# The weight sums of the second feed-forward matmul: DMA adds into the raw tiles in SBUF in place of sums kept in device memory

## Chip, cores, metric

One core of one Trainium2 chip runs the whole program. The metric is device microseconds for one execution; the times given are medians of repeated runs. The engines are TensorE (PE: matmuls, PEld: its weight loads), VectorE (DVE), ScalarE (ACT), GpSimd (POOL) and SyncE (SP). DMAs are issued by SyncE, ACT or GpSimd and carried out by 16 DMA engines.

## What is computed

One decoder block on 512 tokens of width 1024 in float32: normalisation, one input projection, sparse attention beside a gated channel mixer, an output projection with residual, and then the feed-forward part that the change is about:

```python
h = rms_norm(x, g_ffn_norm[l])
x = x + jnp.square(jax.nn.relu(h @ w_ff1[l])) @ w_ff2[l]
```

`w_ff1` is 1024 x 4096, `w_ff2` 4096 x 1024. The output is the new `x`.

## The kernel before

**Precision.** TensorE multiplies in a reduced format, so each operand is split in a high and a low part and each product is three matmuls (`three`, lines 354 to 358: high by high, high by low, low by high). ACT makes the high part with a copy, VectorE the low part by subtracting it from the raw value.

**First feed-forward matmul.** 32 hidden tiles of 128 rows, 24 matmuls each, weights streamed by SyncE into `raw`, four slots of 128x1024. ACT applies the relu from PSUM (`relu`, lines 1012 to 1016), VectorE squares (`square`, line 1529) and makes three sums of the activations of a K-tile pair (`sums`, lines 1536 to 1539). The activations lie in `aq`, six forms of 256 tokens each: A11, S1, A22, S2, A12, A21.

**Second feed-forward matmul.** It is a Strassen-like scheme: K and the tokens are cut in halves, and instead of eight block products there are seven, P1 to P7, of sums of blocks. 16 K-tiles of each half are paired. For a pair k the stored weights `w_ff2[k, 0:4]` are four 128x512 pieces (their signs are such that all sums are additions). With w0 to w3 for them, P1 uses w0, P5 w0+w1, P6 w0+w1+w2, P4 w0+w1+w2+w3, P3 w2, P7 w1+w2, P2 w3. A product has two PSUM banks, one for each 128 tokens: P1 and P2 banks 0 and 1, P5 and P3 2 and 3, P6 and P7 4 and 5, P4 6 and 7.

The sums of weights are made by GpSimd's DMA queue in device memory, in the tensor `forms` (five pieces for a pair): `form_step` (line 570) issues seven DMAs for a pair, three copies and four adding ones, each waiting for the one before on the same pair; two pairs, even and odd, take turns. They start once the mixer's norms are done and run beside attention and the first feed-forward matmul. SyncE then loads the tiles from `forms` or `w_ff2` (`first_group`, `second_group`, lines 464, 472, 475). In step J of the first group one pair is used for P1, P5, P6 and P4: two raw tiles of 1024 columns (P1 and P5, P6 and P4), and four activation forms split in one piece of 1024 columns (`a_high` on ACT, line 1037; `a_low` on VectorE, line 1544), in one of two slots. A step of the second group does P3, P2, P7 of one pair with 1.5 tiles and 768 columns. `fourth_sum` (line 1550) makes the form S4. Between the groups ACT and VectorE keep P1, P5, P6, P4 in `part`; `base` (line 1611) adds what they give to the residual, and `result` (lines 1632, 1636) finishes the rows of `xs`, which SyncE writes out. The last two pairs are interleaved by the table `LAST_TWO`.

**Semaphores.** `raw_in` counts loads, `w_hi` and `w_lo` split weight tiles, `ah_done` and `al_done` split activations, `w_used` tiles that TensorE is through with. A raw slot is free when `w_lo` says so; a slot of the split weights when `w_used` does. TensorE waits for `w_lo` and `al_done` only. All orders are written out by hand.

Of the kernel before, what the change touches and what calls it, by code (L numbers as in the profile page):

```python
# [5 lines left out]
F32 = mybir.dt.float32  # L6
# [6 lines left out]
P = 128  # L13
# [25 lines left out]
FR = 4  # L39
# [17 lines left out]
def ring(n):  # L57
# [14 lines left out]
FIRST = slice(A11, S2 + 1)  # L72
SECOND = slice(S4, S3 + 1)
# [5 lines left out]
LAST_TWO = [("P7", 0, 0), ("P7", 1, 0), ("P3", 0, 0), ("P3", 1, 0), ("P7", 0, 1), ("P7", 1, 1), ("P2", 0, 0),  # L79
            ("P3", 0, 1), ("P3", 1, 1), ("P2", 1, 0), ("P2", 0, 1), ("P2", 1, 1)]  # L80
ENDED = [(p, i) for p, i, e in LAST_TWO if e]
assert len(STREAM) % RAW == 0 and NF % FR == 0 and FR == RAW
# [99 lines left out]
def hybrid_block(nc, x, xt, w512, w_c, cmp_w1, cmp_w2, cmp_pe, sp_w, sp_b, g_cols, g_ffn, g_heads, g_sgu,  # L182
                 g_kc, rope, w_ff1, w_ff2, forms, y):
    ctx = ExitStack()
    with ctx:
# [86 lines left out]
        aq = at("aq", [P, HF, 6, TH], F32, o_a)  # L272
        a_hi = [at("a_hi0", [P, 4, TH], F32R, o_wh + SPARE * UW * 4), at("a_hi1", [P, 4, TH], F32R, o_ht[0])]
        a_lo = [at("a_lo0", [P, 4, TH], F32R, o_wh + (SPARE + 1) * UW * 4), at("a_lo1", [P, 4, TH], F32R, o_ht[0] + 4096)]
# [26 lines left out]
        raw_in = [sem(f"raw_in{i}") for i in range(RAW)]  # L301
        w_hi, w_lo = sem("w_hi"), sem("w_lo")
# [40 lines left out]
        form_made = [sem("form_made_even"), sem("form_made_odd")]  # L343
        p_whole, p1_kept, kept, based = sem("p_whole"), sem("p1_kept"), sem("kept"), sem("based")
# [67 lines left out]
        def _(sp):  # L412
# [55 lines left out]
            def second_group(j, i):  # L468

                k, J = i * 2 + j, i * 2 + (HF + j)  # L470
                sp.wait_ge(w_lo, J * 2 + (NS + NF - RAW + 1))
                sp.dma_start(raw[:, 2 * j, :].rearrange("p (h n) -> p h n", h=2),
                             w_ff2[k, 2:4].rearrange("h p n -> p h n")).then_inc(raw_in[2 * j], 16)
                sp.wait_ge(w_lo, J * 2 + (NS + NF - RAW + 2))
                sp.dma_start(raw[:, 2 * j + 1, 0:512], forms[k, 4]).then_inc(raw_in[2 * j + 1], 16)

            for i in range(HF // 2):
                for j in range(2):
                    sp.wait_ge(form_made[j], 16 * 7 * (i + 1))
                    first_group(j, i)  # L480
            with sp.Fori(0, HF // 2) as i:
                for j in range(2):
                    second_group(j, i)

            sp.wait_ge(final, 1)
            sp.dma_start(y[2], xs[:, 2, :]).then_inc(y_out, 16)
            sp.wait_ge(final, 2)
            sp.dma_start(y[3], xs[:, 3, :]).then_inc(y_out, 16)
            for n, (t, c) in enumerate([(0, slice(512, D)), (1, slice(512, D)), (0, slice(0, 512))]
# [1679 lines left out]
```

## Time and profile before

| | us |
|---|---|
| median of 3 runs | 604.99 (604.17 to 605.15) |
| span of the profiled execution | 602.5 |
| TensorE busy | 591.3 |
| VectorE, ACT, GpSimd busy | 390.1, 300.1, 94.7 |
| DMA moved | 112.51 MB, of it 39.58 MB by GpSimd's queue |

The span is from the first to the last instruction of one profiled execution. A run's time is some 2.5 us longer; the page lists no run time of the profiled execution itself. In the chain of work that ended last TensorE has 84%, almost all of it in lines 356 to 358.

### The profile page before, as it was taken

The page shows a single profiled execution, that of the slowest core. Times are in us where ns is not written, and L with a number is a line of the kernel's source. Part 1 is how long each engine was busy: PE and PEld are TensorE (multiplying, and loading weights), DVE is VectorE, ACT ScalarE, POOL GpSimd, SP SyncE. Part 2 cuts the span into 40 slices and gives each one's busy share as a digit, 9 for nine tenths or more (in the row PEclk, how much of TensorE's full clock was granted, in tenths as well). Part 3 has the DMA queues.
Part 4 walks back from the last instruction along what each step waited for, and adds up shares of the span by engine and source line. Part 5 has one row for each costly group of instructions (what it writes and reads, how often), then busy time and mean ns, then how long its engine had stood idle before and what let it go on. Part 6 is the DMA issues. An engine that isn't in the chain of part 4 may idle for free.

```text
span 602.5 us, 8925 instructions
## 1 busy us (share of the span) xinstructions
PE 591.3 (98%) x3009; PEld 493.9 (82%) x3009; DVE 390.1 (65%) x653; ACT 300.1 (50%) x533; POOL 94.7 (16%) x150
## 2 busy tenths in 40 slices
PE   8999999999999999999999999999999999999997
PEld 7777777888798889988888888888888888888885
DVE  3799862686688576756435444454368777788766
ACT  6865543648466767544322332233345555565561
POOL 1550000122132221222222222220000000000000
PEclk9999999999999999999999999999999999999999
DMA  8924347288787767667888887785335666655563
GB/s 308 328 92 141 95 157 254 88 330 182 207 168 199 157 141 209 106 166 193 225 250 187 246 213 204 253 206 139 105 102 193 194 191 192 174 154 181 190 207 139
DMA packets 33596, 112.51 MB, mean 187 GB/s; under 512 B 4560, under 2 KB 4848, under 8 KB 30752
## 3 DMA queue, kind: packets, MB, share of 16 engines
q1 hardware_dynamic: 28176, 72.56, 36.6%
q0 software_dynamic: 5248, 39.58, 28.1%
q8 instruction: 16, 0.26, 0.2%
q14 instruction: 12, 0.10, 0.0%
q10 hardware_dynamic: 144, 0.00, 0.0%
HBM read 110.03 MB, written 39.85 MB: 249 GB/s over the span
## 4 chain that ended last, share of the span: by engine, by line
PE 84%; DVE 6%; DMA 3%; POOL 2%; issue 2%; ACT 2%; SPq 1%; ACTq 0%; DVEq 0%
PE ps L356 23%; PE ps L358 23%; PE ps L357 23%; PE ps L1953 4%; PE ps L1941 2%; DMA xT<-in_xt 1%; PE ps L1903 1%; PE ps L1812 1%; PE ps L1904 1%; DMA pe_sb<-in_cmp_pe 1%; POOL rope_k L519 1%; PE ps L1669 1%; DVE ht_lo L1123 1%; PE ps L1775 1%; PE ps L1884 1%
## 5 line engine op out<-in xcount | busy, mean ns | idle before, releaser
L356 PE MATMUL ps<-ht_hi,w_hi_sb 128*128 128x512 f32 (+1 forms) x280 | 107.7, 385 | 0.0
L357 PE MATMUL ps<-ht_lo,w_hi_sb 128*128 128x512 f32 (+1 forms) x280 | 107.3, 383 | 0.0
L358 PE MATMUL ps<-ht_hi,w_lo_sb 128*128 128x512 f32 (+1 forms) x280 | 107.3, 383 | 0.0
L1030 ACT ACTIVATE w_hi_sb<-raw 128x1024 fp32r<-128x1024 f32 (+1 forms) x64 | 61.0, 954 | 61.1 <-PE ps L358 61.1
L1556 DVE TENSOR_TENSOR w_lo_sb<-raw,w_hi_sb 128x1024 fp32r<-128x1024 f32 (+1 forms) x64 | 68.5, 1090 | 32.5 <-ACT w_hi_sb L1030 32.3
L358 PE MATMUL ps<-w_hi_sb,a_lo 128*128 128x512 f32 x224 | 87.1, 389 | 0.0
L356 PE MATMUL ps<-w_hi_sb,a_hi 128*128 128x512 f32 x224 | 87.1, 389 | 0.0
L357 PE MATMUL ps<-w_lo_sb,a_hi 128*128 128x512 f32 x224 | 87.1, 389 | 0.0
L356 PE MATMUL ps<-w_hi_sb,ht_hi 128*128 128x512 f32 x192 | 81.6, 425 | 1.7 <-DVE w_lo_sb L1102 0.8
L1529 DVE TENSOR_TENSOR aq<-aq (+1 forms) x32 | 22.2, 693 | 86.3 <-ACT aq L1016 52.0
L358 PE MATMUL ps<-w_hi_sb,ht_lo 128*128 128x512 f32 x192 | 75.3, 392 | 0.0
L357 PE MATMUL ps<-w_lo_sb,ht_hi 128*128 128x512 f32 x192 | 75.0, 391 | 0.0
L570 POOL DMA_DIRECT2D forms<-in_w_ff x80 | 49.4, 621 | 157.0 <-DMA forms<-in_w_ff 121.0
L358 PEld LDWEIGHTS ps<-ht_hi,w_lo_sb 128*128 128x128 f32 x280 | 52.6, 188 | 10.4
L357 PEld LDWEIGHTS ps<-ht_lo,w_hi_sb 128*128 128x128 f32 x280 | 52.6, 188 | 10.3
L356 PEld LDWEIGHTS ps<-ht_hi,w_hi_sb 128*128 128x128 f32 x280 | 52.6, 188 | 10.2
L940 ACT ACTIVATE p_sb<-ps,nmax 128x128 f32<-128x128 f32 (+3 forms) x64 | 33.6, 526 | 39.0 <-DVE nmax L1392 31.1
L356 PEld LDWEIGHTS ps<-w_hi_sb,a_hi 128*128 128x128 f32 x224 | 42.1, 188 | 8.9 <-DVE a_lo L1544 0.2
L357 PEld LDWEIGHTS ps<-w_lo_sb,a_hi 128*128 128x128 f32 x224 | 42.1, 188 | 8.8
L358 PEld LDWEIGHTS ps<-w_hi_sb,a_lo 128*128 128x128 f32 x224 | 42.1, 188 | 8.6
L1953 PEld LDWEIGHTS ps<-v_sb,pt_sb 128*128 128x128 f32 x320 | 43.5, 191 | 4.1 <-issue 0.7
L356 PEld LDWEIGHTS ps<-w_hi_sb,ht_hi 128*128 128x128 f32 x192 | 36.2, 189 | 9.6 <-issue 2.6
(211 smaller groups left out, 922.0 us busy)
## 6 DMA issues: line engine op xcount, KB each, us to landing
raw<-in_w_ff SPq DMA_DIRECT2D x48, 512.0 KB, 4.2
forms<-in_w_ff POOLq DMA_DIRECT2D x32, 512.0 KB, 5.1
raw<-forms SPq DMA_DIRECT2D x32, 512.0 KB, 3.7
forms<-in_w_ff POOLq DMA_DIRECT2D x48, 256.0 KB, 4.9
raw<-in_w SPq DMA_DIRECT2D x23, 512.0 KB, 5.3
forms<-forms POOLq DMA_DIRECT2D x32, 256.0 KB, 5.1
xs<-in_x SPq DMA_DIRECT2D x8, 512.0 KB, 8.4
raw<-in_cmp_w SPq DMA_DIRECT2D x8, 512.0 KB, 4.5
```

The source lines that it names most:

```text
L356: pe.matmul(out, l_hi, r_hi, start=start, stop=False)
L357: pe.matmul(out, l_hi, r_lo, start=False, stop=False)
L358: return pe.matmul(out, l_lo, r_hi, start=False, stop=stop)
L519: pool.tensor_tensor(out, bc(table, shape), bc(g, shape), ALU.mult).then_inc(rope_made, 1)
L570: pool.dma_start(forms[k, out], src, **how).then_inc(form_made[k % 2], 16)
L940: act.activation(p_sb[:, v % 3, 0:n], ps[:, s_no(v) % SBANKS, c:c + n], ACT.Exp, bias=nmax[:, v:v + 1], scale=1.0 if v < PAIRED else -1.0, ...
L1030: act.activation(w_hi_sb[:, FS[slot], 0:n], raw[:, slot, 0:n], ACT.Copy).then_inc(w_hi, 1)
L1123: dve.tensor_tensor(l, src, h.bitcast(F32), ALU.subtract).then_inc(ht_done, 1)
L1529: dve.tensor_tensor(a, a, a, ALU.mult).then_inc(squared, 1)
L1556: dve.tensor_tensor(w_lo_sb[:, FS[slot], 0:n], raw[:, slot, 0:n], w_hi_sb[:, FS[slot], 0:n].bitcast(F32), ALU.subtract).then_inc(w_lo, 1)
L1941: mm = pe.transpose(ps[:, 4 + v % 2, k * P:k * P + P], p_sb[:, v % 3, k * P:k * P + P], ident[:, :])
L1953: mm = pe.matmul(ps[:, 6 + h // 4, c:c + HD], pt_sb[:, v % 3, k * P:k * P + P], v_sb[:, k, b, g * HD:g * HD + HD], start=k == 0, stop=k == t)
```

## The change

The tensor `forms` and its DMAs are gone. The two token halves' K-tiles are now taken as eight pairs k, each with two K-tiles e = 0, 1, and a weight tile of 128x1024 holds one of the four pieces for both K-tiles. The stage is 56 units of one such tile: in a block of four pairs first four units of P1, then four of P5, of P6, of P4; two such blocks; then for each block P3, P7, P2. P1, P3 and P2 tiles are loaded by SyncE. For P5, P6, P4 and P7 GpSimd issues a DMA that adds the next piece into the same raw slot, once the low part of the tile that is there has been made (`raw_added` counts them). Each unit has its own 512 columns of activations, in one of four slots. The last four units are run for the first 128 tokens and then for the second.

```diff
-PRODUCTS = {"P1": (A11, 0, 0, 0), "P5": (S1, 0, 1, 2), "P6": (S2, 1, 0, 4), "P4": (A22, 1, 1, 6),
-            "P3": (S4, 0, 0, 2), "P2": (A12, 0, 1, 0), "P7": (S3, 1, 0, 4)}
-G1, G1_LAST = ["P1", "P5", "P6", "P4"], ["P1", "P6", "P5", "P4"]
-G2, G2_FIRST = ["P3", "P2", "P7"], ["P2", "P3", "P7"]
...
+PRODUCTS = {"P1": (A11, 0), "P5": (S1, 2), "P6": (S2, 4), "P4": (A22, 6), "P3": (S4, 2), "P7": (S3, 4), "P2": (A12, 0)}
+BLOCK = 4
+ROUNDS = ([(p, b, q, q > 0) for b in range(HF // 2 // BLOCK) for q, p in enumerate(["P1", "P5", "P6", "P4"])]
+          + [(p, b, q, p == "P7") for b in range(HF // 2 // BLOCK) for p, q in [("P3", 2), ("P7", 1), ("P2", 3)]])
+NU = BLOCK * len(ROUNDS)
+
+
+def unit(n):
+
+    product, block, q, added = ROUNDS[n // BLOCK]
+    return product, block * BLOCK + n % BLOCK, q, added
...
+FOURTH = {n + 1: unit(n)[1] for n in range(NU) if unit(n)[0] == "P6"}
...
-            def first_group(j, i):
-
-                J = i * 2 + j
-                for unit in range(2):
-                    sp.wait_ge(w_lo, J * 2 + (NS + NF - RAW + 1 + unit))
-                    sp.dma_start(raw[:, 2 * j + unit, :].rearrange("p (h n) -> p h n", h=2),
-                                 forms[J, 2 * unit:2 * unit + 2].rearrange("h p n -> p h n")
-                                 ).then_inc(raw_in[2 * j + unit], 16)
...
+            for n in range(NU):
+                _, k, q, added_up = unit(n)
+                if not added_up:
+                    sp.wait_ge(w_lo, NS + NF + n - RAW + 1)
+                    sp.dma_start(raw[:, n % RAW, :], w_ff2[k, q]).then_inc(raw_in[n % RAW], 16)
...
-            def form_step(k, n):
-
-                out, src, op = [(slice(0, 2), w_ff2[k, 0:2], None), (slice(2, 4), w_ff2[k, 2:4], None),
-                                (1, w_ff2[k, 0], ALU.add), (2, forms[k, 1], ALU.add), (3, forms[k, 2], ALU.add),
-                                (4, w_ff2[k, 1], None), (4, w_ff2[k, 2], ALU.add)][n]
-                how = {} if op is None else {"accum_op": op, "max_dma_last_dim": 8192}
-                pool.dma_start(forms[k, out], src, **how).then_inc(form_made[k % 2], 16)
-
-            for i in range(HF // 2):
-                for n in range(7):
-                    for j in range(2):
-                        if i or n:
-                            pool.wait_ge(form_made[j], 16 * (7 * i + n))
-                        form_step(2 * i + j, n)
+            for n in range(NU):
+                _, k, q, added_up = unit(n)
+                if added_up:
+                    pool.wait_ge(w_lo, NS + NF + n - RAW + 1)
+                    pool.dma_start(raw[:, n % RAW, :], w_ff2[k, q], accum_op=ALU.add, max_dma_last_dim=8192
+                                   ).then_inc(raw_added[n % RAW], 16)
...
+            def unit_hi(n):
+
+                j = n % BLOCK
+                act.wait_ge(w_used, U0 + n - BLOCK + 1)
+                if unit(n)[3]:
+                    act.wait_ge(raw_added[j], 16 * sum(r[3] for r in ROUNDS[:n // BLOCK + 1]))
+                else:
+                    act.wait_ge(raw_in[j], IN1 + 16 * sum(not r[3] for r in ROUNDS[:n // BLOCK + 1]))
+                act.activation(w_hi_sb[:, FS[j], :], raw[:, j, :], ACT.Copy).then_inc(w_hi, 1)
+
+            def a_high(n):
+
+                product, k, _, _ = unit(n)
+                act.wait_ge(w_used, U0 if n < BLOCK and n >= 2 else U0 + n - BLOCK + 1)
+                act.wait_ge(summed, 3 * HF + k + 1 if product == "P3" else 6 * (k + 1))
+                act.activation(a_hi[n % BLOCK][:, :, :], aq[:, k, PRODUCTS[product][0], :, :], ACT.Copy
+                               ).then_inc(ah_done, 1)
 
...
             for j in range(FR):
                 relu((NF // FR - 1, j))
-                form_hi(j, NW + NF - FR + j + 1, IN1 + 16)
-                if j % 2:
-                    a_high(j // 2, j // 2, FIRST, NW + NF - (2, 0)[j // 2], 3 * (j // 2) + 3)
...
+                unit_hi(j)
+                if j < 2:
+                    a_high(j)
+            a_high(2)
+            a_high(3)
+            for n in range(BLOCK, NU):
+                unit_hi(n)
+                a_high(n)
...
             for j in range(FR):
                 square(NF // FR - 1, j)
-                form_lo(j, H0 + j + 1)
-                if j == 1:
-                    sums(NF // FR - 1, 1)
+                unit_lo(j)
                 if j % 2:
-                    a_low(j // 2, j // 2, FIRST, j // 2 + 1)
-            sums(NF // FR - 1, FR - 1)
-            for J in range(2):
-                fourth_sum(J, J + 1)
...
+                    sums(NF // FR - 1, j)
+                    a_low(j // 2)
+            a_low(2)
+            a_low(3)
...
+            for n in range(BLOCK, NU):
+                unit_lo(n)
+                a_low(n)
+                if n in FOURTH:
+                    fourth_sum(n)
...
+            def ready(n):
+
+                pe.wait_ge(al_done, n + 1)
+                pe.wait_ge(w_lo, NS + NF + n + 1)
...
+            for n in range(NU - BLOCK):
+                product, k, _, _ = unit(n)
+                ready(n)
...
+                for e in range(2):
                     for i in range(2):
...
+                        mm = piece(n, e, i)
+                mm.then_inc(w_used, 1)
+            for i in range(2):
+                for n in range(NU - BLOCK, NU):
+                    if i == 0:
+                        ready(n)
+                    for e in range(2):
+                        mm = piece(n, e, i)
+                mm.then_inc(m_done, 1)
```

VectorE's order where the first feed-forward matmul ends and the second begins (`w_lo_sb` is the low part of a weight tile, `aq` to `aq` in pieces of 2x256 a square, in pieces of 256 a sum, `a_lo` the low part of activations). Before:

```order
L1529 TENSOR_TENSOR aq<-aq 128x2x256 [waits bank_free]
L1556 TENSOR_TENSOR w_lo_sb<-raw,w_hi_sb 128x1024 [waits w_hi]
L1544 TENSOR_TENSOR a_lo_102<-aq,a_hi_100 128x1024 [waits ah_done]
L1536 TENSOR_TENSOR aq<-aq 128x256 [waits squared]
L1538 TENSOR_TENSOR aq<-aq 128x256 [waits summed]
L1539 TENSOR_TENSOR aq<-aq 128x256
L1550 TENSOR_TENSOR aq<-aq 128x256 [waits al_done] x2
```

and after the change:

```order
L1489 TENSOR_TENSOR aq<-aq 128x2x256 [waits bank_free]
L1514 TENSOR_TENSOR w_lo_sb<-raw,w_hi_sb 128x1024 [waits w_hi]
L1496 TENSOR_TENSOR aq<-aq 128x256 [waits squared]
L1498 TENSOR_TENSOR aq<-aq 128x256 [waits summed]
L1499 TENSOR_TENSOR aq<-aq 128x256
L1521 TENSOR_TENSOR a_lo_104<-aq,a_hi_100 128x512 [waits ah_done]
L1521 TENSOR_TENSOR a_lo_105<-aq,a_hi_101 128x512 [waits ah_done]
L1521 TENSOR_TENSOR a_lo_106<-aq,a_hi_102 128x512 [waits ah_done]
```

The activations of the second slot stood ahead of the three sums and now stand behind them; `a_lo_104` is unit 1's.

ACT's order from the last weight tile of the first four on. Before:

```order
L1030 ACTIVATE w_hi_sb<-raw 128x1024 [waits raw_in3,w_used]
L1037 ACTIVATE a_hi_100<-aq 128x1024 [waits summed,w_used]
L1030 ACTIVATE w_hi_sb<-raw 128x1024 [waits raw_in0]
L1030 ACTIVATE w_hi_sb<-raw 128x1024 [waits raw_in1,w_used]
L1037 ISA [waits summed]
```

and after:

```order
L1012 ACTIVATE w_hi_sb<-raw 128x1024 [waits raw_in3,w_used]
L1019 ACTIVATE a_hi_101<-aq 128x512 [waits summed,w_used]
L1019 ACTIVATE a_hi_102<-aq 128x512 [waits summed,w_used]
L1012 ACTIVATE w_hi_sb<-raw 128x1024 [waits raw_added0,w_used]
L1019 ACTIVATE a_hi_99<-aq 128x512 [waits summed,w_used]
L1012 ACTIVATE w_hi_sb<-raw 128x1024 [waits raw_added1,w_used]
```

The copies of weights now wait for the adds of the same slot, and each is followed by the activations of its unit.

## Rows read from the trace of the kernel before

**Rows 1.** The page: span, and TensorE's granted clock in tenths, 40 slices.

```profile
span 602.5 us, 8925 instructions
...
PEclk9999999999999999999999999999999999999999
```

**Rows 2.** Stretches: length, busy us (instructions) of each engine, clock, DMA share, GB/s.

```profile
117.00:200.00 83.00, 81.55 (x513) 71.58 (x511) 61.47 (x155) 49.69 (x140) 20.67 (x33) 1.00 0.78 216
200.00:262.00 62.00, 60.32 (x427) 54.41 (x427) 42.55 (x105) 36.41 (x84) 16.93 (x25) 1.00 0.66 142
440.00:515.00 75.00, 75.00 (x332) 62.12 (x332) 54.09 (x58) 41.78 (x43) 0.00 (x0) 1.00 0.57 181
```

**Rows 3.** TensorE's timeline: start, us; first and last matmul of the stage.

```profile
445.93 0.39 PE L356 MATMUL ps<-w_hi_sb,a_hi 128*128 128x512 f32 x1
...
598.04 0.39 PE L358 MATMUL ps<-w_hi_sb,a_lo 128*128 128x512 f32 x1
```

**Rows 4.** GpSimd's longest wait (117 to 300 us), one add in its timeline, SyncE's loads.

```profile
POOL forms L570 <- DMA forms<-in_w_ff: 92.4, 47, 4.8
...
315.96 0.76 POOL L570 DMA_DIRECT2D forms<-forms  x1 [0.77 <-DMA forms<-in_w_ff]
...
L464 SPq DMA_DIRECT2D raw<-forms x32: 367/368/393, 411.0 to 513.8; - x32
```

**Rows 5.** Timelines of ACT and TensorE near 200 us, and the stretch around them.

```profile
201.15 0.58 ACT L940 ACTIVATE p_sb<-ps,nmax 128x384 f32<-128x384 f32 x1
...
201.87 0.55 PE L1941 MATMUL ps<-ident,p_sb 128*128 128x128 f32 x3 [1.22 <-ACT p_sb L940]
...
198.00:203.00 5.00, 3.78 (x25) 3.13 (x24) 1.85 (x7) 4.94 (x11) 0.81 (x2) 1.00 0.67 213
```

**Rows 6.** Groups by shape, 440 to 600 us: busy, mean ns of one, idle before.

```profile
L1556 DVE TENSOR_TENSOR w_lo_sb<-raw,w_hi_sb 128x1024 fp32r<-128x1024 f32 x46 | 56.2, 1224 | 28.7 <-ACT w_hi_sb L1030 28.5
L1030 ACT ACTIVATE w_hi_sb<-raw 128x1024 fp32r<-128x1024 f32 x46 | 48.8, 1061 | 53.1 <-PE ps L358 53.1
...
L1556 DVE TENSOR_TENSOR w_lo_sb<-raw,w_hi_sb 128x512 fp32r<-128x512 f32 x16 | 11.0, 686 | 3.2 <-ACT w_hi_sb L1030 3.2
...
L1611 DVE SCALAR_TENSOR_TENSOR xs<-part,rstd,xs 128x1024 f32<-128x1024 f32 x4 | 5.1, 1280 | 0.0
```

**Rows 7.** VectorE's timeline at the start of the stage.

```profile
447.77 1.23 DVE L1556 TENSOR_TENSOR w_lo_sb<-raw,w_hi_sb 128x1024 fp32r<-128x1024 f32 x1 [0.25 <-ACT w_hi_sb L1030]
448.92 1.22 DVE L1544 TENSOR_TENSOR a_lo<-aq,a_hi 128x1024 fp32r<-128x1024 f32 x1
450.05 0.41 DVE L1536 TENSOR_TENSOR aq<-aq 128x256 f32<-128x256 f32 x1
...
451.18 0.75 DVE L1550 TENSOR_TENSOR aq<-aq 128x256 f32<-128x256 f32 x2
```

**Rows 8.** The page's DMA issues: KB each, median us from issue to landing.

```profile
raw<-in_w_ff SPq DMA_DIRECT2D x48, 512.0 KB, 4.2
...
raw<-forms SPq DMA_DIRECT2D x32, 512.0 KB, 3.7
...
forms<-forms POOLq DMA_DIRECT2D x32, 256.0 KB, 5.1
...
spw_sb<-in_sp_w POOLq DMA_DIRECT2D x1, 512.0 KB, 3.6
```

**Rows 9.** Queues in 316:325, 391:401, 303.6:308.6, 420:440 us: packets, MB, share of 16 engines.

```profile
q0 software_dynamic: 178, 1.01, 63.9%
...
q0 software_dynamic: 192, 1.05, 54.1%
...
q0 software_dynamic: 49, 1.02, 59.5%
...
q1 hardware_dynamic: 878, 1.70, 26.5%
```

**Rows 10.** SyncE's queue in 590 to 602.5 us, in the same columns.

```profile
q1 hardware_dynamic: 1008, 2.10, 43.9%
```

More of the change, by code:

```diff
@@ L1024, in _ @@
             IN1 = IN0 + 16 * (NF // RAW)
-            def form_hi(slot, used, loaded, n=UW):
-                act.wait_ge(w_used, used)
-                act.wait_ge(raw_in[slot], loaded)
-                act.activation(w_hi_sb[:, FS[slot], 0:n], raw[:, slot, 0:n], ACT.Copy).then_inc(w_hi, 1)
-            def a_high(slot, k, pieces, used, sums):
-                act.wait_ge(w_used, used)
-                act.wait_ge(summed, sums)
-                n = pieces.stop - pieces.start
-                act.activation(a_hi[slot][:, 0:n, :], aq[:, k, pieces, :], ACT.Copy).then_inc(ah_done, 1)
@@ L1060, in _ @@
-                if j % 2:
-                    a_high(j // 2, j // 2, FIRST, NW + NF - (2, 0)[j // 2], 3 * (j // 2) + 3)
-            with act.Fori(1, HF // 2) as i:
-                for j in range(2):
-                    first_group(j, i)
-            second_group(0, 0)
-            act.wait_ge(p_whole, 1)
-            act.activation(part[:, :, 0, :], ps[:, 0:2, :], ACT.Copy).then_inc(p1_kept, 1)
-            second_group(1, 0)
-            with act.Fori(1, HF // 2 - 1) as i:
-                for j in range(2):
-                    second_group(j, i)
@@ L1072, in _ @@
-            for j in range(2):
-                second_group(j, HF // 2 - 1, skew=j == 1)
+                unit_hi(j)
[6 more added lines that the diff above has]
+                a_high(n)
+                if n == whole("P1") + BLOCK - 1:
+                    act.wait_ge(w_used, U0 + whole("P1"))
+                    act.activation(part[:, :, 0, :], ps[:, 0:2, :], ACT.Copy).then_inc(p1_kept, 1)
@@ L2038, in _ @@
                     hidden_part(j, range(NK)).then_inc(w_used, 1)
-            def piece(j, product, i, first, last):
-                a, unit, half, bank = PRODUCTS[product]
-                a -= (FIRST if product in G1 else SECOND).start
-                rows, c = slice(i * P, i * P + P), slice(half * 512, half * 512 + 512)
-                return three(pe, ps[:, bank + i, :], a_hi[j][:, a, rows], a_lo[j][:, a, rows],
-                             w_hi_sb[:, FS[2 * j + unit], c], w_lo_sb[:, FS[2 * j + unit], c], first, last)
@@ L2073, in _ @@
-            step(0, 0, G1, first=True)
-            step(1, 1, G1)
-            with pe.Fori(1, HF // 2 - 1) as i:
-                for j in range(2):
-                    step(j, i * 2 + j, G1)
-            step(0, HF - 2, G1)
-            step(1, HF - 1, G1_LAST, last=True)
-            step(0, HF, G2_FIRST, first=True)
-            step(1, HF + 1, G2)
-            with pe.Fori(1, HF // 2 - 1) as i:
-                for j in range(2):
-                    step(j, i * 2 + (HF + j), G2)
-            seen = set()
@@ L2087, in _, with piece @@
-            for n, (p, i, e) in enumerate(LAST_TWO):
-                unit, J = PRODUCTS[p][1], 2 * HF - 2 + e
-                if e not in seen:
-                    pe.wait_ge(al_done, J + 1)
-                    seen.add(e)
-                if (e, unit) not in seen:
-                    pe.wait_ge(w_lo, 2 * J + NS + NF + 1 + (unit if e == 0 else 1 - unit))
-                    seen.add((e, unit))
-                mm = piece(e, p, i, False, e == 1)
-                if e:
-                    mm.then_inc(m_done, 1)
+            def piece(n, e, i):
+                j, (product, k, _, _) = n % BLOCK, unit(n)
+                rows, c = slice(i * P, i * P + P), slice(e * 512, e * 512 + 512)
+                return three(pe, ps[:, PRODUCTS[product][1] + i, :], a_hi[j][:, e, rows], a_lo[j][:, e, rows],
+                             w_hi_sb[:, FS[j], c], w_lo_sb[:, FS[j], c], k + e == 0, k == HF // 2 - 1 and e == 1)
```

196 lines of the change are left out of this document (67 added, 129 removed).

## The prediction

> **What bounds the kernel now.** I read the page's busy line first, then the share by stretch, then TensorE's own timeline. TensorE is busy for all but 11 us of a 602.5 us span (the table), and its granted clock is full (2.4 GHz, the 9s) in all 40 slices [rows 1]. In the attention stage there are still holes (83.0 - 81.55 = 1.4 us and 62.0 - 60.3 = 1.7 us), from 440 us on there are none [rows 2]. The second feed-forward matmul's first matmul starts at 445.93 us and its last at 598.04 us [rows 3]. Its 7 products are 672 matmuls before and after, so the pace is 152.11 / 671 = 0.2267 us. 672 at that pace leave no room for a single wait. So this stage can't become shorter by the change; it can only stay or grow. I call 12 matmuls (one 128x1024 weight tile) a unit: it takes 2.72 us. There are 56 units, and the ring of four tiles turns once in 10.88 us.
>
> **What goes.** 112 DMAs on GpSimd's queue that made the sums in device memory. Nothing but GpSimd itself waited for them (92.4 us in 47 waits for the DMAs from `w_ff2` between 117 and 300 us), and it has no other work there [rows 4]. SyncE reads the first sum at 411.0 us [rows 4]; GpSimd's last DMA is issued before that. The holes of TensorE in the attention stage are not theirs: the largest, 1.22 us before 201.87, ends with an ACT activation [rows 5]. I take the gain of removing them as 0, and let it be at most about half of the 3.1 us of holes, for the range. The 48 loads from the sums become 24 loads by SyncE and 32 adds; bytes moved in the stage shrink, but no one waited for them: ACT's weight copies waited for TensorE (53.1 us) [rows 6].
>
> **What moves: the first units.** This is the term that I find. Before, the activations of a K-tile are split in one piece of 1024 columns, and the piece in slot 1 is needed only after two units (5.44 us). Now each unit has its own 512 columns, so unit 1 needs its a_lo after one unit, at 445.93 + 2.72 = 448.65 us. On VectorE the order row shows that the three sums of the last K-tile are now ahead of that a_lo. The timeline has every step up to there unchanged: the weight split of slot 3 starts at 447.77 and VectorE is free for the next at 448.92 [rows 7], which now are the sums. They took 451.18 - 450.05 = 1.13 us in the trace, so the new a_lo starts at 448.92 + 1.13 = 450.05, lasts about 0.69 us (an estimate from the 128x512 weight split, 686 ns [rows 6]) and is done at 450.74. TensorE starts some 0.14 us after its releaser (ACT's activation ended at 201.73, the matmul started at 201.87 [rows 5]): 450.88. The stall is 450.88 - 448.65 = **2.2 us**, all on the path, since TensorE never idles later and has nothing with which to win it back. Bounds: 1.8 (a release before the recorded end) to 2.5. Units 2 and 3 follow without a wait: their a_lo come 0.6 us apart, TensorE takes 2.72 us for each.
>
> **The steady part.** For each unit ACT has 1.06 us for the weights and less than that for half as many columns of activations, VectorE 1.22 us and 0.69 us [rows 6]: under 2.1 and 1.9 us of 2.72. The eight units with the fourth sum add one operation of 512 columns (two of 256 took 0.75 us [rows 7]), 2.7 us in all, which still fits. The two partial sums at unit 31 and the four base rows at units 36 to 39 (1.28 us each [rows 6]) make VectorE late by some 2 us at most. A unit's halves are ready 0.1 + 1.06 + 1.22 + 0.69 = 3.1 us after TensorE leaves the unit four before it, and needed after 3 x 2.72 = 8.2 us: a cover of 5 us. In the last round TensorE takes the halves of four units in turn, 1.36 us each; the last is ready after about 3.2 us and needed after 4.08. Cost of all this: 0.
>
> **The adds.** This is the unknown: no row shows an add into SBUF. Latency: the add for a tile can start once its weight split is done, 2.4 us after TensorE leaves the unit four before, and has until 10.88 us: 8.5 us for no lateness at all. Adds of 256 KB in device memory took 5.1 us to land, a 512 KB GpSimd load into SBUF 3.6 us, SyncE's loads 3.7 to 4.2 us [rows 8]. A 512 KB add is that load plus a second read, some 1.4 us more of the engines' time (below): 5.0 us, or 6.5 with others queued ahead; I take 5.5. Enough. Throughput: in two stretches with adds only, GpSimd's queue moved 1.01 MB in 63.9% of 9 us (5.75 us of all 16 engines, 176 GB/s) and 1.05 MB in 54.1% of 10 us (194 GB/s); plain copies moved 1.02 MB in 59.5% of 5 us (343 GB/s), plain loads 1.70 MB in 26.5% of 20 us (321 GB/s) [rows 9]. So an add costs 1.8 to 2 times a copy, and one of 0.524 MB takes 2.7 to 3.0 us of the engines, against 2.72 us for a unit. It is at the edge, but it needn't hold for ever: at most 12 adds stand between two rounds of plain loads. In the second block the first add has 3.0 us in hand (10.88 less 5.5 of latency less 2.4), and TensorE waits only when the cover of 5 us is used too: 8.0 us over 12 adds, 0.67 us each. An add may take 3.4 us (154 GB/s) before TensorE waits at all. A round of loads then wins back 10.88 - 3.9 - 2.4 = 4.6 us. GpSimd's issue of an add took 0.76 us with 32 rows [rows 4]; with 128 rows at worst four times that, 3.0 us, under the same limit. I take 0.
>
> The Trainium skill, "Collectives: The Full Stack", section "The bandwidth ceiling: the fold count and why AG ≠ RS ≠ AR", says that a reducing DMA reads two sources for each write and so runs at half a copy's rate. This trace agrees in the ratio (1.8 to 2). "DMA: Bandwidth & Descriptors" in the same skill fits a GpSimd DMA as 2.0 us plus bytes at 436 GB/s; with both reads counted that would be an estimate of 2.4 us of transfer for an add, below a unit, and the sum would be the same; the rows' slower rates make the limit much nearer than the page does.
>
> **The end.** Before, all 2.10 MB of output go out behind the last microseconds of the matmul: 43.9% of 12.5 us, at 380 GB/s without a gap [rows 10]. Now 1.5 MB of it can leave 5 to 20 us earlier, and only the last 256 KB tile is behind the last matmul. VectorE's last three operations are the same. I take 0.4 us off the last landing (0 to 0.8).
>
> **Sum.** 602.5 + 2.2 - 0.4 = 604.3 us of span. The runs shown have a median of 604.99, 2.5 us above the profiled span; with the same 2.5 us it is **606.8 us** (+0.3%). Its own range: 606.0 (a stall of 1.8, 0.8 off the end) to 607.5.
>
> **Rivals.** First, the adds are too slow: slower still. For it: at 2.7 to 3.0 us they have no room in steady state, an add's row is now 4 KB instead of 8 KB, so a fixed cost for each row would count twice, and its destination is read and written in SBUF, which no row prices. Against: the plain loads into SBUF, with 4 KB rows, ran nearly as fast as the copies in device memory (321 and 343 GB/s). It decides from 3.4 us an add. At 4.0 us: in the first block 8 adds count (the first four are issued before the stage begins), 8 x 1.28 - 8.0 = 2.2 us; in the second 12 x 1.28 - 8.0 + 0.4 (the part of the cover that a round of loads doesn't win back) = 7.8 us; the four adds of a P7 round fit in the cover. 606.8 + 10.0 = 617. At 4.5 us: 6.2 + 13.8, so 627.
>
> Second, on the other side: the sums in device memory did cost something in the attention stage. 112 DMAs at a DMA share of 0.66 to 0.78 [rows 2] ran beside weight loads, and ACT's and VectorE's small operations there set when TensorE goes on. If half of the 3.1 us of holes were theirs and the end gains 0.8 us, the kernel comes out at 605.0 + 2.2 - 1.6 - 0.8 = 604.8, no change; it needs all 3.1 us and the 0.8 to reach 603.3. Against: the holes end with ACT and VectorE, not with a DMA. It decides from the point where 1.8 us of holes vanish.
>
> Third, the stall is not what I take it for: were the a_lo of slot 1 needed later, or ready before, the time would be 604.6. The order of instructions speaks against it.
>
> A drop of TensorE's clock after the 2.2 us stall would cost about a microsecond more; the 1.22 us hole before 201.87 left the granted clock at 1.00 [rows 5].
>
> **How the numbers follow.** The forecast has a chance of 0.60, the slow adds 0.25, gains earlier in the kernel 0.10, no stall 0.05. A measurement of this kernel can tell about 0.2% (1.2 us) from no change: below 603.8 is faster, above 606.2 slower. Of the forecast's 0.60 I put 0.50 above and 0.10 within (its low end is 606.0, and the three runs differ by 1 us); the slow adds are all slower; the other two give 0.09 within and 0.06 faster. Slower 0.75, same 0.19, faster 0.06. The range reaches from 604.5, which leaves out the best outcomes of the last two, to 617, which holds the slow adds up to 4.0 us each.
>
> **What would show it.** Right: one gap of TensorE near 448.7 us of 1.8 to 2.5 us, ended by VectorE's a_lo; no other gap until the last matmul near 600.3; adds that land within 8.5 us; a last landing 3.6 us after the last matmul's end. Wrong: ACT's weight copy waiting for a DMA into the raw tiles with TensorE's gaps behind it, growing through P5, P6 and P4 (slow adds); shorter holes between 117 and 262 us (contention that I priced at nothing).

## The result, and the profile after

The changed kernel takes 606.79 us (median of 5 runs, 606.47 to 607.8), the kernel before beside it 604.26 us (5 runs, 604.17 to 605.15): a ratio of 1.0037, with a 95% interval of 1.0025 to 1.005. A second group (12 runs against 35, `again` below) gave 606.53 against 605.04, 1.0026 (1.0015 to 1.0037). The groups of runs of before have medians of 604.26 to 605.16, and within a group its runs lie up to 1.9 us apart, so the larger second group is the better guide: 1.5 us slower by the medians, 1.7 by the means (606.68 against 604.95).

The profiled execution took 607.8 us and has a span of 606.0 us, so 1.8 us lie outside the span. On the page of after, GpSimd's queue and its share are what is left of the sums:

```profile
span 606.0 us, 8433 instructions
...
PE 593.3 (98%) x3009; PEld 495.0 (82%) x3009; DVE 389.5 (64%) x661; ACT 300.4 (50%) x549; POOL 48.6 (8%) x70
...
DMA packets 21698, 74.83 MB, mean 123 GB/s; under 512 B 2640, under 2 KB 2928, under 8 KB 21664
...
q0 software_dynamic: 5248, 18.60, 16.5%
...
L554 POOL DMA_DIRECT2D raw<-in_w_ff x32 | 27.6, 861 | 427.8 <-DVE w_lo_sb L1514 427.8
...
raw<-in_w_ff POOLq DMA_DIRECT2D x32, 512.0 KB, 5.5
```

A third of the bytes of the whole program is gone (112.51 to 74.83 MB), GpSimd's time is half, and the time went up. The stretches say where not to look and where to look. Columns as in [rows 2]:

```profile
117.00:200.00 83.00, 81.55 (x510) 71.46 (x509) 61.85 (x154) 49.15 (x138) 0.57 (x1) 1.00 0.24 84
200.00:262.00 62.00, 60.32 (x429) 54.47 (x428) 42.39 (x105) 36.38 (x85) 0.00 (x0) 1.00 0.06 18
440.00:515.00 75.00, 73.03 (x316) 59.97 (x315) 51.13 (x62) 41.47 (x54) 17.18 (x20) 0.98 0.89 169
```

In the attention stage the share of the DMA engines fell from 0.78 to 0.24 and from 0.66 to 0.06, and TensorE's busy time is that of [rows 2] to the hundredth. From 440 us on it is 73.03 instead of 75.00 us, and the granted clock is 0.98. TensorE's waits in that stage, for engines and DMAs together, are one row (us, times, longest):

```profile
PE ps L366 <- DVE a_lo L1521: 2.0, 1, 2.0
```

TensorE's timeline around it, the counterpart of [rows 3]:

```profile
448.74 0.39 PE L367 MATMUL ps<-w_lo_sb,a_hi 128*128 128x512 f32 x1
448.96 0.39 PE L368 MATMUL ps<-w_hi_sb,a_lo 128*128 128x512 f32 x1
451.32 0.50 PE L366 MATMUL ps<-w_hi_sb,a_hi 128*128 128x512 f32 x1 [1.97 <-DVE a_lo L1521]
451.66 0.45 PE L367 MATMUL ps<-w_lo_sb,a_hi 128*128 128x512 f32 x1
451.91 0.63 PE L368 MATMUL ps<-w_hi_sb,a_lo 128*128 128x512 f32 x1
452.33 0.63 PE L366 MATMUL ps<-w_hi_sb,a_hi 128*128 128x512 f32 x1
...
602.42 0.39 PE L368 MATMUL ps<-w_hi_sb,a_lo 128*128 128x512 f32 x1
```

and VectorE's at the same place, which answers to [rows 7]:

```profile
448.31 1.23 DVE L1514 TENSOR_TENSOR w_lo_sb<-raw,w_hi_sb 128x1024 fp32r<-128x1024 f32 x1 [0.25 <-ACT w_hi_sb L1012]
449.45 0.42 DVE L1496 TENSOR_TENSOR aq<-aq 128x256 f32<-128x256 f32 x1
449.90 0.43 DVE L1498 TENSOR_TENSOR aq<-aq 128x256 f32<-128x256 f32 x1
450.24 0.42 DVE L1499 TENSOR_TENSOR aq<-aq 128x256 f32<-128x256 f32 x1
450.58 1.89 DVE L1521 TENSOR_TENSOR a_lo<-aq,a_hi 128x512 fp32r<-128x512 f32 x3
```

The three sums run from 449.45 to 450.58, and only then comes the a_lo of unit 1, 0.63 us for one of three. At a pace of 0.2267 us TensorE's next matmul was due at 448.96 + 0.23 = 449.19; it starts at 451.32. The hole is 2.13 us. Behind it is something that the kernel before doesn't have: matmuls of 0.63 us that follow each other in 0.43 us (the longest one of its lines 356 to 358 takes 0.50 us). The stretches give the granted clock:

```profile
450.00:451.00 1.00, 0.00 (x0) 0.00 (x0) 1.00 (x3) 0.96 (x2) 0.68 (x1) 1.00 0.00 0
451.00:452.00 1.00, 0.68 (x3) 0.58 (x4) 1.00 (x3) 0.00 (x0) 0.00 (x0) 0.93 0.86 74
452.00:455.00 3.00, 3.00 (x9) 2.32 (x8) 2.28 (x4) 0.00 (x0) 0.85 (x1) 0.50 0.79 150
455.00:456.00 1.00, 1.00 (x6) 0.80 (x5) 0.00 (x0) 0.04 (x1) 0.00 (x0) 0.87 0.59 57
```

The clock is at its lower level (1.2 GHz) for 3.4 us, from about 451.9 to 455.3, while TensorE is fully busy. Summed over the four rows the missing clock is 0.07 + 1.50 + 0.13 = 1.7 us. The stage (first to last matmul) is 602.42 - 446.47 = 155.95 us against 152.11 of [rows 3], 3.84 more: 2.13 of the hole and 1.7 of the clock. At the end 606.0 - 602.42 = 3.58 us follow the start of the last matmul, before 602.5 - 598.04 = 4.46: 0.9 won back. The rest of the difference of the two spans, 0.5 us, lies ahead of the stage, which starts at 446.47 instead of 445.93; the other profiles of after and its variants have it between 445.9 and 447.5, and `before_no_sums` below at 446.85, so it is scatter of the start.

The page gives one execution only. Each run's own mean clock tells the others: of the five runs of after the profiled one has 0.997 and 607.8 us, the others 0.999 to 1.0 and 606.47 to 606.94.

### The profile page after: what moved, and what is told of

Its sections match the earlier page's. It is cut to its first block, busy times and chain, and to the rows that moved or that the text cites. A ratio compares the mean times of both kernels' runs of the same rounds, so it can differ in the third digit from the quotient of the medians.

```text
span 606.0 us, 8433 instructions
## 1 busy us (share of the span) xinstructions
PE 593.3 (98%) x3009; PEld 495.0 (82%) x3009; DVE 389.5 (64%) x661; ACT 300.4 (50%) x549; POOL 48.6 (8%) x70
## 2 busy tenths in 40 slices
DMA packets 21698, 74.83 MB, mean 123 GB/s; under 512 B 2640, under 2 KB 2928, under 8 KB 21664
## 4 chain that ended last, share of the span: by engine, by line
PE 85%; DVE 6%; DMA 3%; POOL 2%; issue 2%; ACT 2%; SPq 1%; DVEq 0%; ACTq 0%
PE ps L366 24%; PE ps L368 23%; PE ps L367 23%; PE ps L1902 4%; PE ps L1890 2%; DMA xT<-in_xt 1%; PE ps L1852 1%; PE ps L1761 1%; PE ps L1853 1%; DMA pe_sb<-in_cmp_pe 1%; POOL rope_k L505 1%; PE ps L1618 1%; DVE ht_lo L1084 1%; PE ps L1724 1%; PE ps L1833 1%
## 5 line engine op out<-in xcount | busy, mean ns | idle before, releaser
L1514 DVE TENSOR_TENSOR w_lo_sb<-raw,w_hi_sb 128x1024 fp32r<-128x1024 f32 x56 | 68.6, 1224 | 34.8 <-ACT w_hi_sb L1012 34.8
L1012 ACT ACTIVATE w_hi_sb<-raw 128x1024 fp32r<-128x1024 f32 x56 | 59.4, 1061 | 61.1 <-PE ps L368 61.0
L554 POOL DMA_DIRECT2D raw<-in_w_ff x32 | 27.6, 861 | 427.8 <-DVE w_lo_sb L1514 427.8
```

The source lines that it names most:

```text
L554: pool.dma_start(raw[:, n % RAW, :], w_ff2[k, q], accum_op=ALU.add, max_dma_last_dim=8192).then_inc(raw_added[n % RAW], 16)
L1012: act.activation(w_hi_sb[:, FS[j], :], raw[:, j, :], ACT.Copy).then_inc(w_hi, 1)
L1514: dve.tensor_tensor(w_lo_sb[:, FS[j], :], raw[:, j, :], w_hi_sb[:, FS[j], :].bitcast(F32), ALU.subtract).then_inc(w_lo, 1)
```

## The experiments

Ratios are to the kernel before in the same group (605.04 us over 35 runs in the first, 605.16 over 27 in the second, 605.04 over 7 in the third).

**The change once more.** No edit.

> The changed kernel once more, beside the kernel before on one chip. The theory of the stall (2.1 us at the second unit, 0.8 us won at the end) expects one gap of TensorE of 2.1 us near 449 us and a difference of 1.3 us to 2.8 us, the larger part only where TensorE's granted clock falls after the gap, as it did in the profile of after (half speed from 451.9 to 455.3 us, 1.7 us lost). If the fall follows from the gap by itself, this profile shows it too; if it depends on where the gap happens to lie, it may be absent. The 0.5 us by which the first 264 us were longer is chance by this theory and should not repeat.

606.53 us (12 runs, 605.5 to 608.84), ratio 1.0026 (1.0015 to 1.0037). The profiled execution, 608.23 us, has the same hole of 1.97 us by the view of waits and matmuls of 0.63 us from 452.70 on. Of the 12 runs, three have a mean clock of 0.997 and take 607.6 to 608.8 us (mean 608.2), nine have 0.999 to 1.0 and take 605.5 to 606.9 (mean 606.2). So the clock falls in some executions only, and where it does the mean is 2.0 us longer.

**Unit 1's activations ahead of everything.** In the changed kernel:

```diff
                 unit_lo(j)
                 if j % 2:
                     sums(NF // FR - 1, j)
-                    a_low(j // 2)
+                if j == 1:
+                    a_low(0)
+                    a_low(1)
             a_low(2)
```

> VectorE makes unit 1's a_lo right after unit 0's, two hidden tiles earlier; all else as after. Theory of the stall: no gap of TensorE from 290 us to the last matmul, the stage 152.1 us from first to last matmul, clock 1.00, and 2.1 to 3.8 us less than after: about 603.5 us, 0.8 us less than before (the end). Rival, the loss lies in the adds or in the new order of units: the time stays within 0.5 us of after.

> The run alow_early once more, as the common ground of this group. 604.4 us within 0.5, ratio to the kernel before 0.998 to 1.000, no gap of TensorE in the second feed-forward matmul, full clock throughout, and 3.6 us from the last matmul to the span's end.

604.42 us (11 runs, ratio 0.9989, 0.9981 to 0.9998) and, in the other group, 604.44 us (11 runs, 0.9989, 0.998 to 0.9998). That is 2.1 us below `again` and 0.6 to 0.7 below the kernel before; the 603.5 us expected stood on a before of 604.3. No TensorE wait is left in the stage; the second profile's row, against 73.03 us at 0.98 in after:

```profile
440.00:515.00 75.00, 75.00 (x333) 62.10 (x332) 54.60 (x67) 43.05 (x56) 18.29 (x23) 1.00 0.91 177
```

Everything else of the change is in this kernel, the 32 adds included. So the place of one a_lo in VectorE's order, behind a weight split and three sums, is the whole of the loss. It is faster than before by 0.1%, with an interval that just excludes 1; only its own variant `outputs_held` is as fast and computes the same.

**Ahead of the sums, but behind the weight split.** As after, with `a_low(1)` between `unit_lo(3)` and its `sums`:

```diff
                 unit_lo(j)
+                if j == 3:
+                    a_low(1)
                 if j % 2:
                     sums(NF // FR - 1, j)
-                    a_low(j // 2)
+                if j == 1:
+                    a_low(0)
```

> VectorE makes unit 1's a_lo behind the last weight split but ahead of the three sums: only the sums' 1.13 us are taken out of its way. Theory: the gap shrinks from 2.1 to 1.0 us; the time is 1.0 us above that of the early a_lo if the clock holds, 604.5 us. If any gap makes the clock fall, 1.7 us more, 606.2 us. Rival (the gap is not what costs): as after.

605.29 us (11 runs, ratio 1.0005, 0.9996 to 1.0013). TensorE's and VectorE's timelines:

```profile
448.66 0.39 PE L368 MATMUL ps<-w_hi_sb,a_lo 128*128 128x512 f32 x1
449.88 0.50 PE L366 MATMUL ps<-w_hi_sb,a_hi 128*128 128x512 f32 x1 [0.84 <-DVE a_lo L1521]
450.22 0.39 PE L367 MATMUL ps<-w_lo_sb,a_hi 128*128 128x512 f32 x1
...
449.15 0.68 DVE L1521 TENSOR_TENSOR a_lo<-aq,a_hi 128x512 fp32r<-128x512 f32 x1
449.75 0.42 DVE L1496 TENSOR_TENSOR aq<-aq 128x256 f32<-128x256 f32 x1
```

The hole is 449.88 - 448.89 = 1.0 us, the stage, whose last matmul starts at 599.40, lasts 153.24 us (1.1 more than without a hole), the clock is full in all 11 runs (1.0), and the time is 0.9 us above the early one's. It lies between the two, which is what a loss by place in the queue asks for.

**The kernel before without the sums in device memory.** The 112 DMAs are left out, SyncE loads pieces of `w_ff2` in place of the sums without waiting for `form_made` (the same is done to the fifth sum, not shown), so P5, P6, P4 and P7 use other weights.

```diff
-            for i in range(HF // 2):
-                for n in range(7):
-                    for j in range(2):
-                        if i or n:
-                            pool.wait_ge(form_made[j], 16 * (7 * i + n))
-                        form_step(2 * i + j, n)
...
-                                 forms[J, 2 * unit:2 * unit + 2].rearrange("h p n -> p h n")
+                                 w_ff2[J, 2 * unit:2 * unit + 2].rearrange("h p n -> p h n")
```

> The kernel before without its 112 DMAs on GpSimd's queue: no sums are made, and SyncE loads the stored pieces in the place of the sums, same sizes and same waits (left out: the weight sums, so the output isn't the reference's). Theory: nothing but GpSimd waited for these DMAs, so the time is that of before within 0.5 us, 604.3 us, and TensorE's busy time in the attention stage is the same. Rival (they cost something beside attention): up to 3.1 us less. A third: the start of the program is 0.5 us longer when GpSimd's queue is short of them, as in the profile of after: 604.8 us.

605.17 us (11 runs, ratio 1.0005, 0.9997 to 1.0014): no gain of more than 0.2 us, and at most 0.8 us of loss.

```profile
117.00:200.00 83.00, 81.55 (x510) 71.55 (x509) 62.26 (x155) 48.77 (x138) 0.57 (x1) 1.00 0.24 84
200.00:262.00 62.00, 60.32 (x429) 54.50 (x428) 42.01 (x105) 36.50 (x84) 0.00 (x0) 1.00 0.05 18
```

The DMA share falls as in after, and TensorE's busy time stays. The sums were hidden, and there was nothing to win by taking them away.

**The adds as plain loads.** The early one, with the sums of weights left out:

```diff
-                    pool.dma_start(raw[:, n % RAW, :], w_ff2[k, q], accum_op=ALU.add, max_dma_last_dim=8192
-                                   ).then_inc(raw_added[n % RAW], 16)
+                    pool.dma_start(raw[:, n % RAW, :], w_ff2[k, q]).then_inc(raw_added[n % RAW], 16)
```

> The early one with GpSimd's 32 adds turned into plain loads of the same bytes into the same raw slots; the sums of weights are left out, so P5, P6, P4 and P7 use other weights. My theory, that the adds in SBUF are never late and cost nothing: the same time as the early one within 0.3 us, and TensorE without a gap in both. Rival: the adds' reading and writing of SBUF slows ACT's or VectorE's reads a little, or delays something at the joints: 0.5 us or more faster than the early one. The landing of a 512 KB DMA by GpSimd should fall from 5.4 us to about 3.6 to 4.

604.44 us (11 runs), the early one's time to the hundredth. The price of an add is there, but hidden. The queues in 500 to 518 us, where the only traffic is GpSimd's (packets, MB, share; then KB each and us to landing), first after, then this kernel:

```profile
q0 software_dynamic: 962, 3.49, 105.4%
...
raw<-in_w_ff POOLq DMA_DIRECT2D x7, 512.0 KB, 5.5
```

```profile
q0 software_dynamic: 980, 3.59, 59.7%
...
raw<-in_w_ff POOLq DMA_DIRECT2D x6, 512.0 KB, 3.7
```

3.49 MB are 6.66 tiles of 0.524 MB in 18 us: one for each unit of 2.7 us, 194 GB/s, as fast as they were asked for. A plain load of 0.524 MB took 59.7% of 18 us over 6.85 tiles, 1.57 us of all 16 engines. The add's share of 105% doesn't give a price in the same way: a share of more than all the engines' time can't be their use alone, so packets must overlap in it, and a queue at 105% was still on time.

**Twice the adds.** The early one; from unit 8 on each add is followed by one more that nobody reads:

```diff
+                    if n >= 2 * BLOCK:
+                        if extra[0] == 0:
+                            pool.wait_ge(w_used, U0)
+                        e, turn = extra[0] % 2, extra[0] // 2
+                        if turn:
+                            pool.wait_ge(extra_added[e], 16 * turn)
+                        how = {"accum_op": ALU.add, "max_dma_last_dim": 8192} if turn else {}
+                        pool.dma_start(spill[:, e, :], w_ff2[k, q], **how).then_inc(extra_added[e], 16)
+                        extra[0] += 1
```

> The early one (no stall at the start) with the adds' work doubled: from unit 8 on, each of the 28 adds is followed by another DMA by GpSimd of the same 512 KB of weights, added into one of two spare tiles in SBUF that nobody reads (the first into each is a plain load). The output is the reference's. It measures what the engines can carry, which the change itself doesn't reach: there GpSimd's queue moved 194 GB/s with one add for each unit of 2.72 us. If an add takes 2.85 us of all 16 engines (the middle of what the sums in device memory gave), two want 5.7 us for a unit: 8 adds of the first block are 8 x 2.98 = 24 us too long, less 8 us of cover, the second block 12 x 2.98 - 8 = 28, the rounds of P7 3 to 8: 45 to 55 us slower than the early one, 650 to 660 us, with ACT's weight copies waiting for the DMA. If an add into SBUF takes 2.4 us: 2 x 2.4 - 2.72 = 2.1 us for each, 9 + 17 + 0 to 3, so some 630 us. If 1.4 us or less (SBUF's second read costs the engines nothing): no change, 604.5.

656.23 us (4 runs, 655.19 to 657.37; ratio 1.0843, 1.0824 to 1.0861). The waits of TensorE and of ACT from 440 us on, GpSimd's timeline in the second block, and its queue in 514 to 523 us:

```profile
PE ps L368 <- DVE a_lo L1533: 32.8, 19, 3.4
...
ACT w_hi_sb L1024 <- DMA raw<-in_w_ff: 92.3, 24, 4.9
...
513.50 0.86 POOL L566 DMA_DIRECT2D spill<-in_w_ff  x1 [3.20 <-DMA spill<-in_w_ff]
...
538.40 0.86 POOL L566 DMA_DIRECT2D spill<-in_w_ff  x1 [3.25 <-DMA spill<-in_w_ff]
...
q0 software_dynamic: 523, 1.88, 106.7%
```

The time falls into the range that was given for 2.85 us an add, but the parts don't. From 513.50 to 538.40 five pairs of adds go through, 4.98 us each: **2.5 us an add** (1.88 MB in 9 us is 209 GB/s). GpSimd waits for the spare tiles there, but an add now lands after 9.7 us (spare) and 11.6 us (raw) instead of 5.5, so some four are under way at any time and each takes longer for it: the queue is kept full. Whether the 16 engines or something else of this queue sets the 2.5 us, no run tells apart. 45 to 55 us were expected, all of them waits behind the adds. The profiled execution took 657.37 us, 52.9 over the early one: 32.8 are TensorE's 19 waits, and its mean clock is 0.971, (1 - 0.971) x 655.6 = 19 us missing. Together they are 51.8, 1 us short. By the same sum as in the expectation, 2.5 us an add gives 10 us in the first block and 19 in the second, and a few in the rounds of P7, which is the size of the 32.8. That the total met the range for 2.85 us an add is luck: the clock filled the gap. So this run shows what slow adds look like (ACT's copies waiting for the DMA, TensorE behind them, and the clock falling as well), and that an add is nearer to 2.5 than to 2.85 us.

**Outputs held back.** The early one, where SyncE issues no output before the fifth of the seven results:

```diff
-                sp.wait_ge(final, 1 + n)
+                sp.wait_ge(final, max(1 + n, 5))
```

> The change with unit 1's activations split early (as in the run alow_early), and SyncE's queue holds every output row back until the fifth of the results, the first one behind the last units' matmuls, is there; all is computed. It tests the term of the end: 0.4 us were forecast, 0.8 us were read between the last matmul and the span's end. If the end is shorter because most of the output leaves earlier, holding it back should put the last landing back to some 2.6 us and the time up by 0.4 to 0.9 us against the early one, so 605.0 to 605.3. Rival: the end is shorter only because VectorE has one row less behind the last matmul; then it is the early one's time, 604.4, within 0.3.

604.28 us (11 runs, ratio 0.9987, 0.9978 to 0.9996): the early one's time. Landing of the last two DMAs in before; the same and SyncE's queue in 594 to 606 us of after; then in 596 to 606 us of this kernel:

```profile
out_y<-xs SPq DMA_DIRECT2D x2, 128.0 KB, 2.6
```

```profile
q1 hardware_dynamic: 720, 1.57, 34.1%
...
out_y<-xs SPq DMA_DIRECT2D x2, 128.0 KB, 1.8
```

```profile
GB/s 393 369 393 393 451 377 442 377 410 426 393 426 393 410 320 393 393 90 0 254 266 266 258 4 0 0 0 0 0 0 0 0 0 0 0 0 0 0 0 0
...
q1 hardware_dynamic: 948, 1.97, 51.8%
```

Nearly all the output now leaves in the last 6 us, nearly as before the change, and the last rows still land in 1.8 us instead of 2.6. The row of GB/s (40 slices of 0.25 us) shows what is different: the queue has drained for a quarter of a us when the last two DMAs come, where [rows 10] had one stream. That the output leaves 5 to 20 us earlier isn't what shortens the end. The expectation's rival, that VectorE has one row less behind the last matmul, isn't it either. VectorE's last operations, before and after:

```profile
596.45 2.90 DVE L1636 SCALAR_TENSOR_TENSOR xs<-ps,rstd,xs 128x512 f32<-128x512 f32 x5
...
602.84 0.88 DVE L1560 SCALAR_TENSOR_TENSOR xs<-ps,rstd,xs 128x256 f32<-128x256 f32 x2 [4.66 <-PE ps L368]
```

They end at 599.35 and 603.72 us, 1.31 and 1.30 us behind the start of the last matmul. What remains is that the earlier rows are through when the last 256 KB come. The hold was a little short of the old end: the first output is issued 4.2 us ahead of the last matmul here, and 2.8 us ahead of it in before (595.25 us). No run held the rows back longer than this, so how much of a lead the end needs stays open.

**A longer hole.** The change as it is, with the last of the three sums made three more times (`repeated` is a semaphore):

```diff
+                for m in range(again):
+                    dve.tensor_tensor(q[S2], q[S1], q[A11], ALU.subtract).then_inc(repeated, 1)
+                    dve.wait_ge(repeated, m + 1)
                 dve.tensor_tensor(q[S2], q[S1], q[A11], ALU.subtract).then_inc(summed, 1)
```

> The change as it is, with the last of the three sums ahead of unit 1's activations made three more times (the same values again), which is some 0.4 us each on VectorE. TensorE's gap should be 2.1 + 1.3 = 3.4 us. My theory, that the gap is on the path in full and that the clock falls to half behind it, for 1.7 us lost: 606.5 + 1.3 = 607.8 us, 608.2 if the clock falls in every run and not only in some. Rival: a longer gap leads to a longer time at half clock, in proportion: 608.8 or more. If the clock's fall were a thing of chance and not of the gap, the profile would show the full clock about as often.

> The run stall_longer once more, for a trace of an execution in which the clock fell: of its six executions five had a mean granted clock of 0.994 to 0.996 and took 609.6 to 611.3 us, and the one whose trace was kept had 0.999 and 607.1. My theory: a stretch of half clock starts within a few us of the end of TensorE's 3.4 us gap near 452 us, and is about twice as long as the 3.5 us of the change itself, since (1 - 0.994) x 609 = 3.6 us against (1 - 0.997) x 606 = 1.8. Rival: the missing clock lies elsewhere in the kernel and has nothing to do with the gap.

> The same kernel a third time, for the same reason; if both traces show a stretch of half clock behind the gap, and of the same length, the length belongs to the gap; if one shows none, the fall comes in some executions only, as the runs' times say.

610.6 us (6 runs, ratio 1.009, 1.0076 to 1.0104), then 609.79 and 609.82 us. The first expectation (607.8 us, 608.2 with the clock falling every time) is missed, and the time lies where its rival had it, at 608.8 or more. The hole is as made: 3.35 us by the wait, 3.5 from the matmul that was due to the one that came. Only one of the eight executions kept the clock (0.999, 607.12 us); the others have 0.994 to 0.997 and 609.55 to 611.25. 607.12 is the early one's 604.4 and 2.7 of the 3.5 us of hole, within the start's scatter; what the others take beyond that is clock. Stretches of the three traces, in the order of the runs (the first kept the clock):

```profile
452.00:458.00 6.00, 5.64 (x25) 4.68 (x26) 4.81 (x8) 1.58 (x2) 0.86 (x1) 1.00 0.61 100
```

```profile
451.00:452.00 1.00, 0.00 (x0) 0.00 (x0) 0.96 (x3) 0.00 (x0) 0.00 (x0) 0.61 1.20 94
...
457.00:458.00 1.00, 1.00 (x4) 0.81 (x3) 0.00 (x0) 0.06 (x1) 0.00 (x0) 0.50 0.73 111
458.00:459.00 1.00, 1.00 (x5) 0.78 (x5) 0.00 (x0) 1.00 (x2) 0.00 (x0) 0.98 0.94 180
```

```profile
454.00:455.00 1.00, 1.00 (x6) 0.78 (x5) 1.00 (x3) 0.00 (x0) 0.00 (x0) 0.91 1.01 201
455.00:456.00 1.00, 1.00 (x4) 0.81 (x3) 1.00 (x2) 0.00 (x0) 0.00 (x0) 0.50 0.31 57
...
458.00:459.00 1.00, 1.00 (x5) 0.82 (x4) 0.18 (x1) 1.00 (x2) 0.00 (x0) 0.88 0.70 115
```

The hole ends at 452.41 us in the second run and at 453.39 in the third. The stretch of half clock starts 1.2 us ahead of that end in one and 1.4 us behind it in the other, and lasts 6.8 and 3.4 us. The same hole gives none, a short one or a long one. The stages of the two (from 446.19 to 604.54, and from 447.17 to 604.57 us) are 6.2 and 5.3 us longer than that of before: 3.5 of hole, and 2.7 and 1.8 of clock. The third run's expectation, one length, is refuted; the second's, that the missing clock lies at the hole and is twice as long there as in after, holds for the second run; for the third only the place does.

## Why the prediction was right, point by point

The forecast was 606.8 us, the measured medians are 606.79 and 606.53. The steps:

**What goes: 0.** Right. `before_no_sums` gives 1.0005, and the holes of TensorE in the attention stage are the same with a DMA share of 0.06. The second rival (the sums cost something) falls with it.

**The first units: 2.2 us.** Right in mechanism and size: 2.13 us in the trace, and in the runs at full clock 606.2 - 604.2 = 1.9 us (means of nine runs of `again` and of eleven of the early one). The steps of VectorE took 1.13 us for the sums, as read from [rows 7], and 0.68 us for an a_lo by itself (the row of `alow_before_sums`), estimated at 0.69. From the a_lo's start to TensorE's next matmul it was 0.74 us, against 0.83 in the sum. `alow_before_sums` gives the half-way point.

**The clock: about a microsecond, left out of the sum.** This is the part that was argued wrongly. The prediction took the clock to be safe, since a hole of 1.22 us had left it at 1.00 [rows 5]; but 1.22 is not 2.13. By runs: no fall in 11 with a hole of 1.0 us (nor in the 33 of the early one and of `outputs_held`, which have no hole), 4 of 17 with 2.1 us, 7 of 8 with 3.4 us. Eleven runs are few: at 4 in 17, eleven without a fall would come about once in twenty. The 69 runs of before in the later groups add to it, with clocks of 0.998 to 1.0 beside the 1.22 us hole of [rows 5]. Where the clock fell it cost 1.7 us by the trace of after, 2.0 by the runs of `again`, and 1.8 and 2.7 by the stages of the two runs with the longer hole, not "about a microsecond". Over all runs of after that is 4/17 x 1.9 = 0.4 us, and that is the size by which it should have been in the sum.

The Trainium skill, "TensorE: Matmul & The Clock Gate", section "HAM oscillation — how this bites in real kernels", puts the danger at idle gaps that are longer than the 2.13 us of after. The runs agree for 1.0 us and don't for 2.1, where the clock fell in 4 of 17 executions; the measurement decides.

**The steady part: 0.** Right: one TensorE wait in the stage, and 75.00 us busy of 75.00 in the early version.

**The adds: 0.** Right, with both terms a little too dear. Landing was estimated at 5.5 us and is 5.5; the latest took 7.8, against the 8.5 of no lateness at all. In the two traces of the early one the latest took 8.1 and 9.3, the second above the 8.5, and TensorE still didn't wait. Their engines' time was put at 2.7 to 3.0 us; `double_adds` gives 2.5, so in steady state an add fits in a unit's 2.72 us by itself and the cover of 5 us is hardly used. GpSimd's issue took 0.86 us and not up to 3.0: it doesn't grow with the rows as the bound had it (0.76 with 32 rows, 0.86 with 128). The first rival would have needed 3.4 us an add; its price was asked for by `double_adds`, and there its mechanism was seen. Its chance of 0.25 was fair for what the rows of before could tell, since none showed an add into SBUF, but the 194 GB/s of [rows 9] were nearer to the truth than the 176.

**The end: -0.4.** Mis-sized, and with a wrong reason. From the start of the last matmul the span goes on for 3.5 to 3.6 us in every trace of after and its variants, and for 4.4 to 4.5 in before and `before_no_sums`: some 0.9 us less, where 0.8 was the upper bound given, and 0.6 to 0.7 in the runs (the early one against before). The prediction's sign, 3.6 us behind the last matmul's end, was too long: it is 3.2. The early leaving of 1.5 MB doesn't make it (`outputs_held`).

**The sum.** 2.2 - 0.4 = 1.8 us over before. Measured: 1.9 of hole, 0.4 of clock, less 0.65 of the end, 1.65. Two errors of a few tenths, a clock left out and an end too small, stand against each other. That 606.8 and 606.79 agree to the hundredth is luck besides: beside the five runs of before (604.26) the difference was 2.5 us, in the larger group 1.5, and 1.8 was forecast. The anchor was right too, though its reading was not: a run is 1.7 to 1.8 us longer than its own span, not 2.5; the profiled execution of before was a fast one, and adding 2.5 us to its span only worked because the sum was tied to the median. Had the 604.99 not been there, the forecast would have been 604.3 + 1.8 = 606.1.

## What to carry to other kernels

When a step is cut in smaller pieces, its deadlines move forward with the size of the piece: look at every queue for what now stands ahead of the first piece, because a first piece that is due after one unit can't stand behind what was harmless when it was due after two. In a stage in which the bounding engine never waits, work that is hidden is worth nothing when it is removed, and each hole costs itself plus, where it is long (2.1 us here; it wasn't seen at 1.0), a chance of the clock falling. A transfer that adds can replace one that loads as long as it takes less of the engines than the bounding engine's unit; ask a run with the adds doubled for the margin, and split what it loses into waits and clock.

## What the runs showed of the hardware

- A DMA that adds 512 KB into SBUF (128 rows of 4 KB) lands in 5.5 us, a plain one by GpSimd in 3.7 to 3.8 us. One went through in 2.5 us (209 GB/s of added data) when the queue was kept full, a plain load in 1.57 us of all 16 engines: a ratio of 1.6, and not the 1.8 to 2 of device memory.
- The share of a queue that adds is shown as 105 to 107% when it is kept busy; 105% at 194 GB/s was not yet the limit.
- TensorE's granted clock fell from 2.4 to 1.2 GHz behind a hole of 2.1 us in 4 of 17 executions and at or behind one of 3.4 us in 7 of 8, never at one of 1.0 us (11 executions). It stayed down for 3.4 us in three of the four traces that show a single fall, and for 6.8 us in the other, of which 1.2 us lay in the hole. In `double_adds`, with 19 holes of up to 3.4 us, 19 us of clock are missing beside 32.8 us of waiting.
